# One matmul of 512 columns for both activation parts in the second half of an expert table, with the two partial results added on VectorE

## The chip, the cores and the metric

The kernel runs on one core of one Trainium2 chip. The metric is the device time of one execution in microseconds (us); the time before is the median of three runs. TensorE has two rows in the profile: PE is the stream of matmuls, PEld the loading of their stationary operands. VectorE is DVE, ScalarE is ACT, GpSimd is POOL, SyncE is SP and issues the DMAs.

## The reference

Two layers of an encoder over 256 positions with 1024 channels. Each layer mixes the positions (attention, a long convolution, a Fourier mixing) and then adds a retrieval of single-neuron experts, which is where most of the time goes. This change touches only the first table of the retrieval, `u_tab`:

```python
s = jnp.einsum('thpd,phkd->thpk', q, sub_keys)      # 8 heads, two halves of 128 keys
...                                                 # top 16 of 16 x 16 pairs: idx, gates g
ue = jnp.take(u_tab, ib, axis=0)
a = jax.nn.gelu(jnp.einsum('thkd,td->thk', ue, xb), approximate=False)
ve = jnp.take(v_tab, ib, axis=0)
return jnp.einsum('thk,thkd->td', (gb * a).astype(ve.dtype), ve)
```

There are 128 x 128 experts. The kernel does not gather: it multiplies all 16384 rows of both tables, and sets the weight of what was not picked to zero.

## The kernel before

Everything is float32, but TensorE is fed in the form fp32r, which keeps fewer bits. So each operand is split in an upper part (`_hi`, a rounded copy made by ScalarE) and a lower part (`_lo`, the original minus the upper part), and each product is three matmuls: upper by lower, upper by upper, lower by upper. The fourth, lower by lower, is left out.

**Tiles.** One layer streams 296 tiles of weights, of 128 x 1024 elements, through four slots `raw`. ScalarE copies each half tile (128 x 512) to `tab_hi`, and GpSimd or VectorE subtracts it to give `tab_lo`. `tab_hi` and `tab_lo` have two slots each, so half a tile can be split as soon as TensorE has used the same half of the tile two before it (semaphore `half_used`). Tiles 40 to 167 of the stream are the 128 tiles of the first table (`u_tile`), the last 128 those of the second (`v_product`).

**A tile of the first table.** Its result is 128 experts by 256 positions. For each of 8 blocks of 128 channels, `u_tile` issues a matmul of `x_lo` and two of `x_hi`, each with a moving operand of 256 columns; all add up in one half of a bank of PSUM (`ps`). Two tiles (a pair) fill a bank. ScalarE then applies GELU to the pair (`gelu` into `work`, from tile 48 on `gelu_in_place` in PSUM).

**The gate stage, tiles 48 to 111.** By tile 48 the picks are known. Between the tiles TensorE makes the gates out of one-hot matrices, four positions at a time: 64 groups, one after each tile (`gates`; 4 float32 matmuls, shown as x8, in a bank of their own). Their operands come from VectorE (`hot_rows` L1586, `hot_columns` L1591 for every second group) and from ScalarE (`distances` L1110 and `one_hot_j` L1118 for the others). VectorE multiplies each finished group into `work` (`weigh_group`, L1598), and multiplies each pair after its GELU into `work` too (`gate_pair`, L1606). GpSimd makes `tab_lo` (`u_lower`, L1239). In what follows a tile whose number in a quad is even opens a pair, and an odd one closes it.

**The tail, tiles 112 to 127.** No gates are made, and VectorE makes `tab_lo` (L1567). The second table follows at once: `v_product` waits for `w_lo` (L1660) of its tile, then for `tab_lo` (L1652). Both stand in one queue on VectorE, behind everything issued before.

Every engine runs its own instructions in the order in which they are written, with semaphores between them. No scheduler decides anything. In the gate stage ScalarE's order for a pair is: distances, split of the two halves of the even tile, one-hot, split of the two halves of the odd tile, GELU of the pair that ended last.

## Time and profile before

| | |
|---|---|
| median of 3 runs | 2057.51 us (2055.43 to 2057.92) |
| the profiled execution | 2052.14 us, span 2050.3 us |
| PE busy | 1958.4 us, 96% of the span |
| PEld busy | 1786.3 us, 87% |
| DVE busy | 1320.7 us, 64% |
| ACT busy | 1103.0 us, 54% |
| POOL busy | 770.4 us, 38% |

A matmul's duration is from its start to its modelled end, and neighbours overlap; how fast matmuls follow each other is read from their starts. In layer 0 the gate stage lies at about 381 to 622 us of the span, the tail at 622 to 668, the second table at 668 to 1023; layer 1 repeats this.

### The profile page before, as it was taken

To read this page: it belongs to the slowest core of one execution; us is meant where nothing else is said; L and a number is where in the kernel's file an instruction comes from. 1 tells how busy PE (TensorE), PEld (TensorE's weight loads), DVE (VectorE), ACT (ScalarE), POOL (GpSimd) and SP (SyncE) were. 2 spreads that over 40 slices of the span, in tenths; PEclk is the share of its full clock that TensorE was granted. 3 is DMA by queue.
4 is the path that set the end of the run, shared out by engine and by line. 5 is a ranking of instruction groups with operands and counts; after the bars stand their busy time and mean duration, and the time that the engine had idled before them with its cause. 6 is when DMAs were issued, how large, how long until landed. Compare 5 with 4: busy or idle time off the path is not lost.

```text
span 2050.3 us, 43061 instructions
## 1 busy us (share of the span) xinstructions
PE 1958.4 (96%) x12792; PEld 1786.3 (87%) x12792; DVE 1320.7 (64%) x2869; ACT 1103.0 (54%) x2124; POOL 770.4 (38%) x553
## 2 busy tenths in 40 slices
PE   7989998999999999999998999989999999999997
PEld 6779997999999887888777799979999998878886
DVE  4655699666666665666546557986666666656665
ACT  4344454666665554555533454546666555555554
POOL 4433599576770000000054316995777600000000
PEclk9999999999999999999999999999999999999999
DMA  5215454444344556555522154544343455565555
GB/s 209 74 42 174 153 178 144 153 143 140 137 142 173 187 194 235 192 194 194 185 73 82 55 182 150 179 145 151 134 143 135 141 178 191 194 244 194 194 190 179
DMA packets 90470, 327.05 MB, mean 160 GB/s; under 512 B 10400, under 2 KB 11168, under 8 KB 89760
## 3 DMA queue, kind: packets, MB, share of 16 engines
q1 hardware_dynamic: 90400, 326.18, 46.0%
q8 instruction: 36, 0.59, 0.1%
q14 instruction: 34, 0.28, 0.0%
HBM read 325.09 MB, written 1.05 MB: 159 GB/s over the span
## 4 chain that ended last, share of the span: by engine, by line
PE 88%; DVE 5%; issue 3%; POOL 2%; DMA 1%; ACT 1%; SPq 1%; DVEq 0%; POOLq 0%; ACTq 0%
PE ps L795 12%; PE ps L796 12%; PE ps L797 12%; PE ps L868 11%; PE ps L871 11%; PE ps L870 11%; PE ps L814 6%; PE ps L768 2%; PE ps L771 1%; PE ps L770 1%; POOL tab_lo L1239 1%; DVE work L1345 1%; DMA raw<-tab_v 1%; PE ps L579 1%; PE ps L545 1%
## 5 line engine op out<-in xcount | busy, mean ns | idle before, releaser
L1239 POOL TENSOR_TENSOR tab_lo<-raw,tab_hi 128x512 fp32r<-128x512 f32 x416 | 586.3, 1425 | 262.0 <-ACT tab_hi L1071 181.2
L795 PE MATMUL ps<-x_lo,tab_hi 128*128 128x256 f32 x2048 | 591.8, 289 | 22.1 <-POOL tab_lo L1239 18.9
L797 PE MATMUL ps<-x_hi,tab_lo 128*128 128x256 f32 x2048 | 579.1, 283 | 0.0
L796 PE MATMUL ps<-x_hi,tab_hi 128*128 128x256 f32 x2048 | 579.0, 283 | 0.0
L1652 DVE TENSOR_TENSOR tab_lo<-raw,tab_hi 128x512 fp32r<-128x512 f32 x512 | 354.2, 692 | 280.0 <-ACT tab_hi L1166 276.2
L1071 ACT ACTIVATE tab_hi<-raw 128x512 fp32r<-128x512 f32 x504 | 317.5, 631 | 338.9 <-PE ps L797 334.4
L795 PEld LDWEIGHTS ps<-x_lo,tab_hi 128*128 128x128 f32 x2048 | 392.0, 191 | 25.7 <-POOL tab_lo L1239 25.4
L868 PE MATMUL ps<-tab_lo,w_hi 128*128 128x512 f32 x1024 | 400.6, 391 | 7.5 <-DVE w_lo L1660 7.5
L870 PE MATMUL ps<-tab_hi,w_hi 128*128 128x512 f32 x1024 | 399.8, 390 | 0.0
L871 PE MATMUL ps<-tab_hi,w_lo 128*128 128x512 f32 x1024 | 399.8, 390 | 0.0
L796 PEld LDWEIGHTS ps<-x_hi,tab_hi 128*128 128x128 f32 x2048 | 392.5, 192 | 0.0
L797 PEld LDWEIGHTS ps<-x_hi,tab_lo 128*128 128x128 f32 x2048 | 391.9, 191 | 0.0
L1166 ACT ACTIVATE tab_hi<-raw 128x512 fp32r<-128x512 f32 x512 | 319.0, 624 | 103.6 <-PE ps L871 92.8
L868 PEld LDWEIGHTS ps<-tab_lo,w_hi 128*128 128x128 f32 x1024 | 193.3, 189 | 49.0 <-DVE tab_lo L1652 9.2
L871 PEld LDWEIGHTS ps<-tab_hi,w_lo 128*128 128x128 f32 x1024 | 193.1, 189 | 40.5
L870 PEld LDWEIGHTS ps<-tab_hi,w_hi 128*128 128x128 f32 x1024 | 193.3, 189 | 40.1
L1156 ACT ACTIVATE w_hi<-work 128x256 fp32r (+1 forms) x256 | 106.8, 417 | 199.9 <-PE ps L871 198.5
L1598 DVE TENSOR_TENSOR work<-ps,work 128x512 f32 (+1 forms) x128 | 88.6, 692 | 157.3 <-PE ps L814 157.3
L1187 POOL TENSOR_TENSOR small<-small,kc 128x2 f32<-128x2 f32 x10 | 6.9, 692 | 451.9 <-DVE small L1279 434.8
L895 ACT ACTIVATE tab_hi<-raw 128x512 fp32r<-128x512 f32 (+1 forms) x168 | 100.3, 609 | 131.4 <-PE ps L771 47.4
L1586 DVE TENSOR_SCALAR onehot<-kc,picks 128x128 f32<-128x128 f32 x512 | 168.2, 388 | 0.6
L1194 POOL TENSOR_TENSOR tab_lo<-raw,tab_hi 128x512 fp32r<-128x512 f32 (+1 forms) x96 | 121.5, 1277 | 117.8 <-ACT tab_hi L895 116.5
(204 smaller groups left out, 2527.5 us busy)
## 6 DMA issues: line engine op xcount, KB each, us to landing
raw<-tab_u SPq DMA_DIRECT2D x256, 512.0 KB, 3.2
raw<-tab_v SPq DMA_DIRECT2D x256, 512.0 KB, 3.2
raw<-w_proj SPq DMA_DIRECT2D x68, 512.0 KB, 3.5
raw<-w_proj SPq DMA_DIRECT2D x16, 384.0 KB, 3.1
work<-cdft SPq DMA_DIRECT2D x3, 1536.0 KB, 9.5
work<-cfilter SPq DMA_DIRECT2D x3, 768.0 KB, 5.4
work<-sub_keys SPq DMA_DIRECT2D x2, 1024.0 KB, 5.5
work<-pmat SPq DMA_DIRECT2D x3, 352.0 KB, 6.2
```

The lines of the kernel that those rows point to most:

```text
L795: mm(bank, hi, x_lo[:, 4 * h + k, :], start=(h + k == 0), stop=False)
L796: mm(bank, hi, x_hi[:, 4 * h + k, :], start=False, stop=False)
L797: last = mm(bank, lo, x_hi[:, 4 * h + k, :], start=False, stop=(h + k == 4))
L814: last = mm(ps[:, 2 + s, t * P:(t + 1) * P], onehot[:, s % 2, 0, t, :], onehot[:, s % 2, 1, t, :], start=True, stop=True)
L868: mm(bank, w_hi[:, s % 2, tok], lo, start=(first and s == 0), stop=False, skip_group_check=True)
L870: mm(bank, w_hi[:, s % 2, tok], hi, start=False, stop=False, skip_group_check=True)
L871: last = mm(bank, w_lo[:, s % 2, tok], hi, start=False, stop=last_tile, skip_group_check=True)
L1071: fn(half(tab_hi, s, h), half(raw, s, h), ACT.Copy).then_inc(hi_done.sem, 1)
L1166: fn(half(tab_hi, s, h), half(raw, s, h), ACT.Copy).then_inc(hi_done.sem, 1)
L1239: tt(half(tab_lo, s, h), half(raw, s, h), half(tab_hi, s, h).bitcast(F32), ALU.subtract).then_inc(lo_pool.sem, 1)
L1586: last = v.tensor_scalar(onehot[:, slot, 0, t, :], iota, picks[:, 0, bass.ds(n * 4 + t, 1)], picks[:, 2, bass.ds(n * 4 + t, 1)], ALU.is_eq ...
L1652: v.tensor_tensor(half(tab_lo, s, h), half(raw, s, h), half(tab_hi, s, h).bitcast(F32), ALU.subtract).then_inc(lo_dve.sem, 1)
```

## The change

For tiles 48 to 127 the upper part of the table is multiplied with both activation parts in one matmul. `x_hi` and `x_lo` become two views of one tensor `x_hl`, in which the 256 upper and 256 lower columns of a channel block lie side by side. The result of the 512 columns fills a whole bank: the left half holds the upper product, and the product of `tab_lo` with `x_hi` is added there, while the right half holds the product with `x_lo`. The two halves have to be added, which a new step `sum_pair` does on VectorE for each pair, out of PSUM into a new SBUF tensor `sums`. GELU then works in `sums` and waits for that step; `gate_pair` reads `sums` instead of PSUM and is moved one tile later. A pair takes two banks (0 and 1, or 2 and 3), and the gates go to banks 4 to 7.

```diff
-        x_hi = sb("x_hi", [P, DT, SEQ], F32R)
-        x_lo = sb("x_lo", [P, DT, SEQ], F32R)
+        x_hl = sb("x_hl", [P, DT, 2, SEQ], F32R)
...
+        sums = sb("sums", [P, 2, 2, SEQ])
...
+                def u_tile_joint(i, s, signal, offset):
+
+                    j = i * 4 + s
+                    for h in range(2):
+                        pe.wait_ge(*at(signal, l, j * 2 + offset + h + 1))
+                        for k in range(4):
+                            col = slice(k * P, (k + 1) * P)
+                            hi, lo = half(tab_hi, s, h)[:, col], half(tab_lo, s, h)[:, col]
+                            mm(ps[:, s, :], hi, x_hl[:, 4 * h + k, :, :].rearrange("p a t -> p (a t)"),
+                               start=(h + k == 0), stop=False, skip_group_check=True)
+                            last = mm(ps[:, s, 0:256], lo, x_hi[:, 4 * h + k, :], start=False, stop=(h + k == 4),
+                                      skip_group_check=True)
+                        last.then_inc(half_used.sem, 1)
...
-                        if s % 2 == 0:
-                            pe.wait_ge(*at(gated, l, i * 2 + s // 2 - 1 - GATE0 // 2))
-                        u_tile(i, s, lo_dve, LO_T)
+                            pe.wait_ge(*at(summed, l, i * 2 + s // 2 - 1 - GATE0 // 2))
+                        u_tile_joint(i, s, lo_dve, LO_T)
...
                 def gelu_in_place(n, bank):
-                    act.wait_ge(*at(half_used, l, n * 4 + 2 * U0 + 4))
-                    fn(ps[:, bank, :], ps[:, bank, :], ACT.Gelu).then_inc(gelu_done.sem, 1)
+                    act.wait_ge(*at(summed, l, n - GATE0 // 2 + 1))
+                    fn(sums[:, bank, :, :], sums[:, bank, :, :], ACT.Gelu).then_inc(gelu_done.sem, 1)
...
+                def sum_pair(n, bank):
+
+                    dve.wait_ge(*at(half_used, l, n * 4 + 2 * U0 + 4))
+                    v.tensor_reduce(sums[:, bank, :, :],
+                                    ps[:, 2 * bank:2 * bank + 2, :].rearrange("p k (a t) -> p k t a", a=2),
+                                    AX.X, ALU.add).then_inc(summed.sem, 1)
...
                         if s == 0 and not first:
+                            sum_pair(i * 2 - 1, 1)
+                        if s == 1 and not first:
                             gate_pair(i * 2 - 1, 1, n)
                             dve.wait_ge(*at(gated, l, i * 2 - GATE0 // 2))
                         if s == 2:
+                            sum_pair(i * 2, 0)
+                        if s == 3:
                             gate_pair(i * 2, 0, n)
                             dve.wait_ge(*at(gated, l, i * 2 + 1 - GATE0 // 2))
...
-                        if s % 2:
+                        if s % 2 == 0:
+                            sum_pair(i * 2 + s // 2 - 1, (s // 2 + 1) % 2)
+                        else:
                             gate_pair(i * 2 + s // 2 - 1, (s // 2 + 1) % 2, GROUPS)
...
                 dve.wait_ge(*at(weighted, l, GROUPS))
+                sum_pair(63, 1)
                 v_quad(0, True)
```

In the order of instructions this stands as follows. VectorE in the first quad of the gate stage, before: the work of three groups, where `work<-ps,work 128x128x4` is `weigh_group` and `work<-ps,work 128x512` is `gate_pair`.

```order
L1598 TENSOR_TENSOR work<-ps,work 128x128x4
L1586 TENSOR_SCALAR onehot<-kc,picks 128x128 x4
L1591 TENSOR_TENSOR onehot<-kc,picks 128x512
L1603 REGISTER_ALU
L1606 TENSOR_TENSOR work<-ps,work 128x512
L1623 ISA
L1596 REGISTER_ALU
L1598 TENSOR_TENSOR work<-ps,work 128x128x4
L1586 TENSOR_SCALAR onehot<-kc,picks 128x128 x4
L1596 REGISTER_ALU
L1598 TENSOR_TENSOR work<-ps,work 128x128x4
```

The same place after the change; line numbers are 16 higher, and `sums<-ps` is `sum_pair`.

```order
L1614 TENSOR_TENSOR work<-ps,work 128x128x4
L1602 TENSOR_SCALAR onehot<-kc,picks 128x128 x4
L1607 TENSOR_TENSOR onehot<-kc,picks 128x512
L1619 REGISTER_ALU
L1620 TENSOR_REDUCE sums<-ps 128x512
L1612 REGISTER_ALU
L1614 TENSOR_TENSOR work<-ps,work 128x128x4
L1602 TENSOR_SCALAR onehot<-kc,picks 128x128 x4
L1626 REGISTER_ALU
L1629 TENSOR_TENSOR work<-sums,work 128x512
L1649 ISA
L1614 TENSOR_TENSOR work<-ps,work 128x128x4
```

The sum has taken the place of `gate_pair` behind the one-hot columns, and `gate_pair` stands one group later. VectorE where the tail ends and the second table begins, before: the last split of the tail, then the first tile of the second table, then the last `gate_pair`.

```order
L1567 TENSOR_TENSOR tab_lo<-raw,tab_hi 128x512
L1603 ISA
L1606 ISA
L1606 TENSOR_TENSOR work<-ps,work 128x512
L1646 REGISTER_ALU
L1646 COMPARE_AND_BRANCH
L1650 REGISTER_ALU
L1651 REGISTER_ALU
L1652 TENSOR_TENSOR tab_lo<-raw,tab_hi 128x512
```

And after the change:

```order
L1583 TENSOR_TENSOR tab_lo<-raw,tab_hi 128x512
L1626 ISA
L1629 ISA
L1629 TENSOR_TENSOR work<-sums,work 128x512
L1674 REGISTER_ALU
L1674 COMPARE_AND_BRANCH
L1619 REGISTER_ALU
L1620 TENSOR_REDUCE sums<-ps 128x512
L1678 REGISTER_ALU
L1679 REGISTER_ALU
L1680 TENSOR_TENSOR tab_lo<-raw,tab_hi 128x512
```

The sum of the last pair, which waits for the end of tile 127, now stands ahead of both splits of the second table's first tile and of its `w_lo`.

## Rows read from the trace of the kernel before

**Rows 1.** The page: busy us and share of each engine.

```profile
PE 1958.4 (96%) x12792; PEld 1786.3 (87%) x12792; DVE 1320.7 (64%) x2869; ACT 1103.0 (54%) x2124; POOL 770.4 (38%) x553
```

**Rows 2.** Chain that ended last, layer 0's gate stage: start us, us, what.

```profile
384.00 0.89 PE ps L814 x8
...
621.29 0.89 PE ps L814 x8
```

**Rows 3.** Timeline of PE, tail and second table: start us, us, line.

```profile
654.78 0.28 PE L795 MATMUL ps<-x_lo,tab_hi 128*128 128x256 f32 x1
...
657.66 0.28 PE L795 MATMUL ps<-x_lo,tab_hi 128*128 128x256 f32 x1
...
672.23 0.40 PE L868 MATMUL ps<-tab_lo,w_hi 128*128 128x512 f32 x1
...
674.96 0.39 PE L868 MATMUL ps<-tab_lo,w_hi 128*128 128x512 f32 x1
```

**Rows 4.** Timeline, gate stage: one pair, and ScalarE's rows of another.

```profile
508.87 0.58 ACT L1102 ACTIVATE ps<-ps 128x512 f32<-128x512 f32 x1
...
510.78 0.63 ACT L1071 ACTIVATE tab_hi<-raw 128x512 fp32r<-128x512 f32 x1
...
546.54 0.58 ACT L1102 ACTIVATE ps<-ps 128x512 f32<-128x512 f32 x1
...
546.61 0.36 PE L795 MATMUL ps<-x_lo,tab_hi 128*128 128x256 f32 x1
...
546.98 0.69 DVE L1598 TENSOR_TENSOR work<-ps,work 128x512 f32 x1 [1.81 <-PE ps L814]
...
548.33 0.63 ACT L1071 ACTIVATE tab_hi<-raw 128x512 fp32r<-128x512 f32 x1
...
548.78 0.68 DVE L1591 TENSOR_TENSOR onehot<-kc,picks 128x512 f32<-128x512 f32 x1
...
549.03 1.56 POOL L1239 TENSOR_TENSOR tab_lo<-raw,tab_hi 128x512 fp32r<-128x512 f32 x1 [1.03 <-ACT tab_hi L1071]
...
549.38 0.68 DVE L1606 TENSOR_TENSOR work<-ps,work 128x512 f32 x1
```

**Rows 5.** Groups by line and form: the reductions of VectorE.

```profile
L1556 DVE TENSOR_REDUCE chosen<-work 128x128 f32<-128x2048 f32 x8 | 18.3, 2286 | 0.3
...
L1376 DVE TENSOR_REDUCE small<-ps 128x4 f32<-128x1024 f32 x8 | 9.8, 1220 | 1.5 <-PE ps L657 1.3
```

**Rows 6.** Timeline of POOL, gate stage: one split, and two in a row.

```profile
500.07 1.28 POOL L1239 TENSOR_TENSOR tab_lo<-raw,tab_hi 128x512 fp32r<-128x512 f32 x1 [0.94 <-ACT tab_hi L1071]
...
503.83 2.83 POOL L1239 TENSOR_TENSOR tab_lo<-raw,tab_hi 128x512 fp32r<-128x512 f32 x2 [1.03 <-ACT tab_hi L1071]
```

**Rows 7.** Chain, 346 to 352 us: GpSimd's slowest split and PE behind it.

```profile
347.60 3.32 POOL tab_lo L1239
...
350.96 0.38 PE ps L795
```

**Rows 8.** Timeline of ACT, tail: last split of a pair's end, then GELU.

```profile
656.78 0.63 ACT L1071 ACTIVATE tab_hi<-raw 128x512 fp32r<-128x512 f32 x1 [0.81 <-PE ps L797]
...
657.32 0.58 ACT L1102 ACTIVATE ps<-ps 128x512 f32<-128x512 f32 x1
```

**Rows 9.** Timeline where the second table begins.

```profile
667.00 0.42 DVE L1660 TENSOR_TENSOR w_lo<-work,w_hi 128x256 fp32r<-128x256 f32 x1
...
667.98 0.28 PE L797 MATMUL ps<-x_hi,tab_lo 128*128 128x256 f32 x1
...
668.10 0.40 PE L868 MATMUL ps<-tab_lo,w_hi 128*128 128x512 f32 x1
...
671.43 0.49 PE L868 MATMUL ps<-tab_lo,w_hi 128*128 128x512 f32 x1 [0.43 <-DVE w_lo L1660]
```

**Rows 10.** Windows: busy us (instructions) by engine, granted clock, DMA share, GB/s.

```profile
802.00:806.00 4.00, 3.08 (x7) 2.48 (x8) 2.28 (x5) 1.15 (x4) 0.00 (x0) 0.50 0.65 230
806.00:812.00 6.00, 6.00 (x22) 4.79 (x21) 2.41 (x4) 2.65 (x6) 0.00 (x0) 0.78 0.25 83
```

More of the change, by code:

```diff
@@ L123, in hybrid_encoder @@
         dist_abs = sb("dist_abs", [P, 4, P])
+        sums = sb("sums", [P, 2, 2, SEQ])
         ps = ctx.enter_context(nc.psum_tensor("ps", [P, 8, 512], F32))
+        x_hi, x_lo = x_hl[:, :, 0, :], x_hl[:, :, 1, :]
         workf = work[:, :, :].rearrange("p j t -> p (j t)")
@@ L311, in hybrid_encoder @@
         unit_set = sig("unit_set", 3)
+        summed = sig("summed", (P - GATE0) // 2)
         gated = sig("gated", (P - GATE0) // 2)
@@ L813, in gates @@
                     for t in range(4):
-                        last = mm(ps[:, 2 + s, t * P:(t + 1) * P], onehot[:, s % 2, 0, t, :],
+                        last = mm(ps[:, 4 + s, t * P:(t + 1) * P], onehot[:, s % 2, 0, t, :],
                                   onehot[:, s % 2, 1, t, :], start=True, stop=True)
@@ L820, in u_gates @@
                         if s % 2 == 0:
-                            if first:
-                                pe.wait_ge(*at(gelu_done, l, i * 2 + s // 2 - 1))
-                            else:
-                                pe.wait_ge(*at(gated, l, i * 2 + s // 2 - 1 - GATE0 // 2))
-                        u_tile(i, s, lo_pool, LO_G)
+                            if not first:
+                                pe.wait_ge(*at(summed, l, i * 2 + s // 2 - 1 - GATE0 // 2))
+                            elif s == 0:
+                                pe.wait_ge(*at(gelu_done, l, i * 2))
+                        u_tile_joint(i, s, lo_pool, LO_G)
                         gates(i, s, first)
@@ L830, in u_tail @@
                         if s % 2 == 0:
-                            pe.wait_ge(*at(gated, l, i * 2 + s // 2 - 1 - GATE0 // 2))
-                        u_tile(i, s, lo_dve, LO_T)
+                            pe.wait_ge(*at(summed, l, i * 2 + s // 2 - 1 - GATE0 // 2))
+                        u_tile_joint(i, s, lo_dve, LO_T)
                 u_product(0, True, lo_pool, LO_E)
@@ L1605, in gate_pair @@
                     pair = work[:, bass.ds(2 * n, 2), :]
-                    v.tensor_tensor(pair, ps[:, bank, :].rearrange("p (k t) -> p k t", k=2), pair, ALU.mult)\
-                        .then_inc(gated.sem, 1)
+                    v.tensor_tensor(pair, sums[:, bank, :, :], pair, ALU.mult).then_inc(gated.sem, 1)
                 def gate_quad(i, first=False, last=False):
@@ L1626, in gate_quad @@
                             u_lower_half(i + 1, 0, 1)
-                        weigh_group(n, 2 + s)
+                        weigh_group(n, 4 + s)
                 hot_rows(0, 0)
@@ L1794 @@
     from concourse.bass_utils import run_bass_kernel_spmd
-    nc = bacc.Bacc("TRN2", target_bir_lowering=False, num_devices=1)
+    nc = bacc.Bacc("TRN2", target_bir_lowering=False, num_devices=1, dynamic_dma_scratch_size=1024)
     arrays = layouts(inputs)
```

## The prediction

> **What bounds the kernel now.** I read the page first. PE is busy for 96% of the span, DVE for 64% and POOL for 38% [rows 1], so TensorE is the first suspect. A busy PE is not yet a bound one, so I then followed the chain that ended last through the gate stage. It never leaves PE there: the gates of the 64 groups start from 384.00 to 621.29, 63 steps of 3.767 us [rows 2], so a pair of tiles takes 7.53 us. What such a period is made of I took from the starts of matmuls, not from their durations. In the tail nine groups of three lie within eight gaps, from 654.78 to 657.66: 24 matmuls of 256 columns in 2.88 us, 0.120 each. In the second table 12 matmuls of 512 columns take 2.73 us, 0.2275 each [rows 3]. A tile of 24 matmuls is therefore 2.88 us and the gates after it 0.89. Last I read the timeline of one pair, to see what each other engine does between the end of a pair and the start of the next but one [rows 4]. That decides this case.
>
> **What TensorE saves.** For each channel block two matmuls of 256 columns (0.240) become one of 512 (0.2275), and the third stays at 0.120. The saving is 0.0125 to 0.0135 us; I take 0.0133, since 256 columns at 0.120 and 512 at 0.227 lie on one line whose fixed part is 0.0133 a matmul. That is 8 x 0.0133 = 0.107 us a tile, and 17.0 us for 160 tiles (80 in each layer) if nothing else moves. A pair in the gate stage would take 7.53 - 0.21 = 7.32.
>
> The trace's cadence is weighed here against a rule. The Trainium skill, "TensorE: Matmul & The Clock Gate", section "Back-to-back issue gap", puts the gap at N/2.4 + 2.5 ns, so that a matmul saved would be worth only 2.5 ns and the change would save 3 us instead of 17. This case's trace has 0.120 for 256 columns where that rule gives 0.109. I go by the trace.
>
> **What VectorE gets.** 80 sums of 1024 values read from PSUM. The nearest row is a reduction of 1024 PSUM values to 4 in 1.220 us; one of 2048 values to 128 takes 2.286 [rows 5], so the price follows the values read, not the results. This one writes 512 results where the rows write 4 and 128. Bounds: 0.69, what an operation with 512 results takes [rows 4], and 2.29, the row with twice the values. I take 1.22, whose row has the values and the memory that this one has. VectorE has room for it: it waits 1.81 before one of the two groups of each pair [rows 4].
>
> **The new chain.** The sum itself is hidden from TensorE, whose banks it frees more than a tile early. But GELU now waits for it, and behind GELU in ScalarE's queue stand the distances and then the split of the even tile of the pair after next, for which GpSimd and then TensorE wait. Before, GELU ran the moment the pair was done: it starts 0.54 after the last split starts [rows 8], at 546.54 in the pair I follow, ahead even of the next tile's first matmul at 546.61 [rows 4]. Now, counted from that first matmul:
> - the gate group is weighed at 546.98, and what follows the one-hot columns of 548.78 starts at 549.38 [rows 4]: the sum starts at +2.77
> - sum 1.22, hand-over 0.03 (an estimate: the hand-over of GpSimd to TensorE below is 0.04): GELU starts at +4.02
> - from the start of GELU to the start of the split 1.79 (546.54 to 548.33) in one pair and 1.91 (508.87 to 510.78) in the next [rows 4], mean 1.85: split at +5.87
> - split 0.63 and 0.07 to the start on GpSimd (548.33 to 549.03) [rows 4]: +6.57
> - GpSimd 1.28 [rows 6]: +7.85
> - TensorE takes over 0.04 later (347.60 + 3.32 = 350.92, PE at 350.96) [rows 7]: the even tile of the pair after next can start at +7.89.
>
> So from the end of pair p to the start of pair p+2 there are 7.89 us, and that pair takes 7.32. The second half of that tile comes a little late too: two splits in a row take 2.83 [rows 6], which ends it at 6.57 + 2.83 = +9.40, and TensorE is through with the first half (four blocks at 0.227 + 0.120 = 0.347, 1.39) at +9.28, so 0.12. Two periods last 7.89 + 7.32 + 0.12 = 15.33, one 7.665 us, against 7.53 before. TensorE's gain of 0.21 is eaten by a wait of 0.345, and each pair is 0.132 slower.
>
> **The other places.** In each layer the first two pairs of the gate stage have no late GELU before them and keep their gain, 2 x 0.21 = 0.43. The tail's 16 tiles keep theirs, 1.71: after the end of an odd tile (656.78, when its last split can start [rows 8]) the sum ends 1.25 later and GELU starts; the split it delays is wanted only 5.5 us after. Splits there are on VectorE, 0.69 each, and fit.
>
> At the start of the second table VectorE's queue now has the last sum ahead of both splits and `w_lo`. Before, `w_lo` was started at 667.00, a us before tile 127 ended, and the second table began at 668.10, 0.12 after the last matmul of the first [rows 9]. Now the sum starts when that matmul ends, 667.98 + 0.28 + 0.04 = 668.30, and after it come two splits and `w_lo`: 1.22 + 2 x 0.61 + 0.42 = 2.86, TensorE at about 671.2, that is 3.1 later. Its second tile starts at 671.2 + 2.73 = 673.9, where before it started at 671.43 after a wait of its own [rows 9]: the cost is 2.5.
>
> Bank 0 of the gate stage now waits for the last GELU of the stage before at once; the picks, which TensorE waits for anyway, come later than that, so it costs nothing. Were that cover gone, it would be part of one GELU, 0.58 [rows 4]. The wider `x_hl` changes no matmul elsewhere: each still reads 256 columns that lie together.
>
> **The sum.** Per layer: 30 pairs x 0.132 = +4.0, -0.43, -1.71, +2.5, so +4.3; two layers +8.6. The profiled execution of 2052.1 (span 2050.3, 1.8 around it; 5.4 under the median of the runs) would become 2060.7, and the median of 2057.5 becomes 2066.1. I say 2066. A measurement of this kernel can tell about 0.2%, 4.1 us.
>
> **The rivals.**
> - *The chain is shorter, and TensorE's gain comes through (faster).* Each 0.1 us off the chain is 0.05 a pair, 3.0 us over 60 pairs. If the sum cost 0.69, by results, a pair would take 7.40 and the total be -7.8 in the 60 pairs, -0.9 in the other four, -3.4 in the tails, +4.0 at the starts of the second table, -8.1: 2049.5. If the chain dropped out altogether (0.69 off), -13.6 - 3.4 + 5.0 = -12: 2045.5. The change turns from loss to gain where the chain is 0.29 shorter, at a sum of 0.93 us. For it: the chain is put together from rows of other places, and some of it may overlap. Against it: the row for 1024 values from PSUM is exact. Chance 0.15.
> - *The chain is 0.15 to 0.42 shorter (no change within 0.2%).* 2053.5 to 2061.5, worked out in the same way. Chance 0.10.
> - *GpSimd is slowed by what now runs beside it.* `gate_pair` reads both inputs from SBUF where one came from PSUM, and it starts near +5.95, right before GpSimd's split at +6.57; also GpSimd now works where the one-hot columns are built. In the rows GpSimd took 1.56 instead of 1.28 for a split that began during the columns [rows 4, 6], and 3.32 at worst beside long operations of VectorE [rows 7]. 0.28 more in the chain is +8.4: 2074.5; a whole 0.68 is +20: 2086. It decides once GpSimd's first split is late by 0.1. Chance 0.15. The Trainium skill, "SBUF — State Buffer", section "Who interferes with whom", says that such an instruction of VectorE and one of GpSimd that reads SBUF exclude each other, and that a reduction never does; by that rule the new form of `gate_pair` is a new rival for GpSimd and the sum is not, and the 1.56 agrees that columns do slow it.
> - *The clock falls at the start of the second table.* The new gap is 3.1 us. After the long wait for a DMA in the second table of layer 0 the granted clock was 0.50 in one window and 0.78 in the next, which is 1.2 GHz for the first and part of the second, and 29 matmuls ran in 10 us [rows 10] where 44 fit: 15 x 0.2275 = 3.4 us lost. Twice, +6.8: 2073. Chance 0.10.
>
> A sum of 2.29 would be 1.07 more in the chain, +32, with +2 at the starts of the second table: 2100. It has no row that speaks for it and no chance of its own here. By the Trainium skill's issue gap a pair in the gate stage would take 7.49 without waits and 7.75 with them, and the kernel would end at about 2075 (an estimate from that page).
>
> **How the numbers follow.** Forecast 0.50, own range 2060 to 2072 (0.06 of it within 0.2%); rivals 0.15, 0.10, 0.15, 0.10. Faster: 0.15 + 0.02 = 0.17. Within 0.2%: 0.06 + 0.08 = 0.14. Slower: 0.44 + 0.15 + 0.10 = 0.69. The range leaves out the fastest half of the first rival and the slow end of the third: 2052 to 2079.
>
> **What would show it.** In the profile after: starts of the joint matmul and the next 0.227 apart, then 0.120; 160 reductions of about 1.22; gates every 7.6 to 7.7 us per pair; PE idle some 0.35 per pair before the first matmul of even tiles, released by GpSimd's `tab_lo`, some 20 us in all; GELU about 4 us after the next tile's start; tail tiles at 2.77; a wait of about 3 us for `w_lo`, twice. The prediction is wrong if PE has no wait in the gate stage (then it is faster), or if GpSimd's mean there rises well over the 1.3 of single splits.

## The result, and the profile after

The changed kernel takes 2161.88 us (median of 4 runs, 2159.32 to 2167.99) where the kernel before takes 2056.47 beside it (4 runs, 2055.11 to 2057.92): 1.0517 times as long, 95% interval 1.0493 to 1.0541. Slower was forecast, but by 0.4%, not by 5.2%; 2161.88 lies far outside 2052 to 2079.

First the page of the changed kernel: busy us and share of the span by engine.

```profile
PE 1968.4 (91%) x11512; PEld 1726.4 (80%) x11512; DVE 1578.0 (73%) x2949; ACT 1077.0 (50%) x2124; POOL 749.3 (35%) x553
```

PE has 1280 matmuls fewer than in [rows 1], as the change says. VectorE has 80 instructions more, but is busy for 257 us more, where 80 sums of 1.22 make 98. The other 159 must be in instructions that were there before. The page's costliest groups say which (busy us, mean ns of one, then idle time before them and who ended it):

```profile
L810 PE MATMUL ps<-x_hl,tab_hi 128*128 128x512 f32 x1280 | 465.9, 405 | 97.5 <-POOL tab_lo L1255 93.9
...
L1602 DVE TENSOR_SCALAR onehot<-kc,picks 128x128 f32<-128x128 f32 x512 | 344.3, 732 | 0.8
...
L1118 ACT ACTIVATE sums<-sums 128x512 f32<-128x512 f32 x80 | 50.7, 633 | 318.8 <-DVE sums L1620 318.8
```

L1602 is `hot_rows`, which builds the one-hot rows for the gates and which the diff doesn't touch. Before, the page has it as L1586:

```profile
L1586 DVE TENSOR_SCALAR onehot<-kc,picks 128x128 f32<-128x128 f32 x512 | 168.2, 388 | 0.6
```

388 ns became 732 in the mean, and that is 176 us more of VectorE (other groups give 16 us back). The sum itself costs what it should; this is its group by form:

```profile
L1620 DVE TENSOR_REDUCE sums<-ps 128x512 f32<-128x1024 f32 x80 | 97.1, 1214 | 22.2 <-PE ps L812 22.2
```

The timeline of one pair in the gate stage shows where the rows lose it. VectorE first (start us, us, engine, line):

```profile
506.10 4.37 DVE L1602 TENSOR_SCALAR onehot<-kc,picks 128x128 f32<-128x128 f32 x4
510.38 0.68 DVE L1607 TENSOR_TENSOR onehot<-kc,picks 128x512 f32<-128x512 f32 x1
510.98 1.21 DVE L1620 TENSOR_REDUCE sums<-ps 128x512 f32<-128x1024 f32 x1
...
512.72 1.10 DVE L1602 TENSOR_SCALAR onehot<-kc,picks 128x128 f32<-128x128 f32 x4
...
520.24 1.21 DVE L1620 TENSOR_REDUCE sums<-ps 128x512 f32<-128x1024 f32 x1
```

Then ScalarE and GpSimd over the same stretch:

```profile
502.98 0.63 ACT L1118 ACTIVATE sums<-sums 128x512 f32<-128x512 f32 x1 [4.85 <-DVE sums L1620]
503.51 1.27 ACT L1126 ACTIVATE dist_abs<-kc,chosen 128x128 f32<-128x128 f32 x4
504.69 1.13 ACT L1087 ACTIVATE tab_hi<-raw 128x512 fp32r<-128x512 f32 x2
...
506.25 1.14 ACT L1087 ACTIVATE tab_hi<-raw 128x512 fp32r<-128x512 f32 x2
...
512.23 0.63 ACT L1118 ACTIVATE sums<-sums 128x512 f32<-128x512 f32 x1 [4.85 <-DVE sums L1620]
```

```profile
505.38 5.00 POOL L1255 TENSOR_TENSOR tab_lo<-raw,tab_hi 128x512 fp32r<-128x512 f32 x4 [4.25 <-ACT tab_hi L1087]
```

Four rows take 1.10 when GpSimd is idle (512.72) and 4.37 when it splits the table (506.10), and the instruction behind the slow four starts at 510.38, the moment GpSimd's run of four splits ends. In shorter windows the view shows them one by one:

```profile
506.61 1.29 POOL L1255 TENSOR_TENSOR tab_lo<-raw,tab_hi 128x512 fp32r<-128x512 f32 x1
506.66 1.32 DVE L1602 TENSOR_SCALAR onehot<-kc,picks 128x128 f32<-128x128 f32 x1
...
507.90 1.33 DVE L1602 TENSOR_SCALAR onehot<-kc,picks 128x128 f32<-128x128 f32 x1
```

A row that starts 0.05 after a split ends with that split, 1.32 later instead of 0.33. So a run of splits without a gap holds one row after the other. In the kernel before, four rows took 1.17 to 1.36 in the same stretch:

```profile
506.18 1.33 DVE L1586 TENSOR_SCALAR onehot<-kc,picks 128x128 f32<-128x128 f32 x4
```

Its splits came singly or in twos [rows 6]. The two that began at 503.83 ended at 506.66, and of the four rows only the first was held, for 0.57.

The three lists close into a ring (each link is released by the one before, and the last releases the first), which I read off by starts: GELU at 502.98, GpSimd 2.40 later, behind the distances and the first split of ScalarE; its run, 5.00; the columns after it, 0.60; the sum and the hand-over to the next GELU, 1.25. That is 9.25, with no time left over: it is the distance from GELU to GELU (502.98 to 512.23) and from sum to sum (510.98 to 520.24). A pair takes 9.25 where it took 7.53 [rows 2]. TensorE only follows. In the list of waits (us in total, times, longest)

```profile
PE ps L810 <- POOL tab_lo L1255: 93.9, 60, 1.9
```

it waits 60 times, about once a pair, as ScalarE waited 80 times for the sum, 318.8 us in all (the third row of the groups above). In windows of the same 211 us (busy us by engine, in the order PE, PEld, DVE, ACT, POOL, then granted clock, DMA share, GB/s) VectorE was at 140.9 before, in the first line, and is at 205.6 now, in the second. It is hardly ever free, and is held for 3.27 of each 9.25 us (4.37 less 1.10):

```profile
409.00:620.00 211.00, 211.00 (x1795) 211.00 (x1794) 140.91 (x337) 133.79 (x276) 146.89 (x110) 1.00 0.40 139
...
409.00:620.00 211.00, 174.32 (x1093) 153.53 (x1092) 205.60 (x298) 101.32 (x230) 113.59 (x91) 1.00 0.34 112
```

Outside the gate stage most went as forecast. In the tail the sums are 5.55 us apart, 2.775 a tile. TensorE then waits 2.93 for the second table, and behind that comes what only a rival had: the granted clock, 1.00 through the gate stage and the tail, is at 0.50 (1.2 GHz). Timeline and windows at the start of the second table in layer 0:

```profile
683.35 1.23 DVE L1620 TENSOR_REDUCE sums<-ps 128x512 f32<-128x1024 f32 x1 [1.31 <-PE ps L812]
688.90 1.23 DVE L1620 TENSOR_REDUCE sums<-ps 128x512 f32<-128x1024 f32 x1 [1.31 <-PE ps L812]
...
716.63 1.23 DVE L1620 TENSOR_REDUCE sums<-ps 128x512 f32<-128x1024 f32 x1 [2.51 <-PE ps L812]
...
718.98 0.42 DVE L1688 TENSOR_TENSOR w_lo<-work,w_hi 128x256 fp32r<-128x256 f32 x1
719.53 0.79 PE L884 MATMUL ps<-tab_lo,w_hi 128*128 128x512 f32 x1 [2.93 <-DVE w_lo L1688]
```

```profile
719.50:723.00 3.50, 3.47 (x8) 2.80 (x9) 2.04 (x4) 0.88 (x2) 0.00 (x0) 0.50 0.66 176
723.00:726.30 3.30, 3.30 (x10) 2.54 (x10) 0.97 (x2) 1.05 (x3) 0.00 (x0) 0.59 0.34 132
726.30:730.00 3.70, 3.70 (x18) 3.05 (x17) 2.27 (x5) 1.88 (x4) 0.00 (x0) 1.00 0.38 144
```

Matmuls of 512 columns start 0.427 apart for 6.1 us, so some 14 of them cost 0.2 more each, 2.9 us. In layer 1 the gap is 2.93 again, and the slow starts end after 3.7 us (1794.19 to 1797.89): some 9 matmuls, 1.7 us.

The account of the two profiled executions (2162.92 against 2052.14, +110.8), from starts on TensorE: first gates to last gates of layer 0 took 287.5 (383.07 to 670.55) against 237.3 (383.83 to 621.13), +50.2; from there to the second table 48.98 against 46.97, +2.0, in which the tail gives back its 1.7, so that the gap and what is late around it cost 3.7; then 2.9 for the clock. That is 55.1. In layer 1 the gates took 288.0 (1457.18 to 1745.21) against 237.3, the way to the second table is the same 48.98, and the clock cost 1.7: 54.4. Together that is 109.5 of the 110.8.

### The profile page after: what moved, and what is told of

Read it like the earlier page. It is cut to its first block, busy times and chain, and to the rows that moved or that the text cites. A ratio compares the mean times of both kernels' runs of the same rounds, so it can differ in the third digit from the quotient of the medians.

```text
span 2160.9 us, 40655 instructions
## 1 busy us (share of the span) xinstructions
PE 1968.4 (91%) x11512; PEld 1726.4 (80%) x11512; DVE 1578.0 (73%) x2949; ACT 1077.0 (50%) x2124; POOL 749.3 (35%) x553
## 4 chain that ended last, share of the span: by engine, by line
PE 63%; DVE 22%; issue 6%; DVEq 2%; ACT 2%; POOL 2%; DMA 1%; SPq 0%; POOLq 0%; ACTq 0%
DVE onehot L1602 12%; PE ps L884 10%; PE ps L886 10%; PE ps L887 10%; PE ps L797 4%; PE ps L799 4%; PE ps L798 4%; PE ps L810 3%; DVE sums L1620 3%; PE ps L812 2%; ACT sums L1118 2%; DVE work L1629 2%; PE ps L770 1%; PE ps L773 1%; PE ps L772 1%
## 5 line engine op out<-in xcount | busy, mean ns | idle before, releaser
L1255 POOL TENSOR_TENSOR tab_lo<-raw,tab_hi 128x512 fp32r<-128x512 f32 x416 | 565.5, 1387 | 388.5 <-ACT tab_hi L1087 307.5
L810 PE MATMUL ps<-x_hl,tab_hi 128*128 128x512 f32 x1280 | 465.9, 405 | 97.5 <-POOL tab_lo L1255 93.9
L1087 ACT ACTIVATE tab_hi<-raw 128x512 fp32r<-128x512 f32 x504 | 301.1, 622 | 175.9 <-PE ps L799 147.8
L1182 ACT ACTIVATE tab_hi<-raw 128x512 fp32r<-128x512 f32 x512 | 319.2, 624 | 106.3 <-PE ps L887 96.0
L810 PEld LDWEIGHTS ps<-x_hl,tab_hi 128*128 128x128 f32 x1280 | 240.3, 188 | 160.9 <-POOL tab_lo L1255 109.1
L812 PE MATMUL ps<-x_hl,tab_lo 128*128 128x256 f32 x1280 | 358.0, 280 | 0.0
L1602 DVE TENSOR_SCALAR onehot<-kc,picks 128x128 f32<-128x128 f32 x512 | 344.3, 732 | 0.8
L812 PEld LDWEIGHTS ps<-x_hl,tab_lo 128*128 128x128 f32 x1280 | 241.6, 189 | 0.0
L797 PE MATMUL ps<-x_hl,tab_hi 128*128 128x256 f32 x768 | 219.2, 285 | 18.9 <-POOL tab_lo L1255 18.9
L798 PE MATMUL ps<-x_hl,tab_hi 128*128 128x256 f32 x768 | 217.3, 283 | 0.0
L799 PE MATMUL ps<-x_hl,tab_lo 128*128 128x256 f32 x768 | 217.2, 283 | 0.0
L1118 ACT ACTIVATE sums<-sums 128x512 f32<-128x512 f32 x80 | 50.7, 633 | 318.8 <-DVE sums L1620 318.8
L797 PEld LDWEIGHTS ps<-x_hl,tab_hi 128*128 128x128 f32 x768 | 147.3, 192 | 21.9 <-POOL tab_lo L1255 21.7
```

Source lines behind the costliest of these rows:

```text
L797: mm(bank, hi, x_lo[:, 4 * h + k, :], start=(h + k == 0), stop=False)
L798: mm(bank, hi, x_hi[:, 4 * h + k, :], start=False, stop=False)
L799: last = mm(bank, lo, x_hi[:, 4 * h + k, :], start=False, stop=(h + k == 4))
L810: mm(ps[:, s, :], hi, x_hl[:, 4 * h + k, :, :].rearrange("p a t -> p (a t)"), start=(h + k == 0), stop=False, skip_group_check=True)
L812: last = mm(ps[:, s, 0:256], lo, x_hi[:, 4 * h + k, :], start=False, stop=(h + k == 4), skip_group_check=True)
L1182: fn(half(tab_hi, s, h), half(raw, s, h), ACT.Copy).then_inc(hi_done.sem, 1)
```

## The experiments

The first theory after reading this: the rows are held by GpSimd's splits because both read SBUF (*the lock*), and the ring feeds on it. The rival: it is my own chain, only longer, or plain load on VectorE.

**rows_from_psum.** The 128 numbers that every one-hot row is compared with are put in a PSUM bank, and `hot_rows` reads them there. To free a bank, the gates of all four groups of a quad use banks 4 and 5 in turn.

```diff
+                v.tensor_copy(ps[:, 6, 0:P], iota)
...
-                        last = v.tensor_scalar(onehot[:, slot, 0, t, :], iota, picks[:, 0, bass.ds(n * 4 + t, 1)],
+                        last = v.tensor_scalar(onehot[:, slot, 0, t, :], ps[:, 6, 0:P], picks[:, 0, bass.ds(n * 4 + t, 1)],
...
-                        weigh_group(n, 4 + s)
+                        weigh_group(n, 4 + s % 2)
```

> The changed kernel, but VectorE's one-hot rows read their 128 columns of iota from a PSUM bank instead of SBUF (so the gates use two banks in turn instead of four). Lock theory (in the changed kernel each of the four row operations of a group waits until GpSimd has ended a split, because both want the same SBUF port): with one input in PSUM the four rows take 1.0 to 1.5 us again instead of 4.4, a pair in the gate stage takes 7.6 to 7.9 us instead of 9.25, and the kernel 2062 to 2085 us. Queue theory (VectorE's queue and the late GELU alone make the period, the long rows are only the place where the wait shows): rows stay long, pair 9.2, kernel about 2160.

2079.78 us (2 runs; before 2052.61), ratio 1.0133 [1.0103, 1.0162]: three quarters of the loss are gone. The gates' use of two banks instead of four was not run alone; it gives VectorE no work and takes none away, and gelu_behind_both below does without it. Groups and timeline of this kernel:

```profile
L1603 DVE TENSOR_SCALAR onehot<-ps,picks 128x128 f32<-128x128 f32 x512 | 173.9, 402 | 0.8
...
L1608 DVE TENSOR_TENSOR onehot<-kc,picks 128x512 f32<-128x512 f32 x64 | 73.4, 1146 | 0.0
```

```profile
506.47 5.45 POOL L1255 TENSOR_TENSOR tab_lo<-raw,tab_hi 128x512 fp32r<-128x512 f32 x4 [2.44 <-ACT tab_hi L1087]
508.39 1.37 DVE L1603 TENSOR_SCALAR onehot<-ps,picks 128x128 f32<-128x128 f32 x4
509.68 1.11 DVE L1608 TENSOR_TENSOR onehot<-kc,picks 128x512 f32<-128x512 f32 x1
510.20 1.72 POOL L1255 TENSOR_TENSOR tab_lo<-raw,tab_hi 128x512 fp32r<-128x512 f32 x1
```

GpSimd still runs its four splits in one piece (506.47 to 511.92), and the rows in the middle of them take 1.37. So the run of splits by itself does not cost the 5%; rows that read SBUF beside it do. The columns, which read two inputs from SBUF, now fall into the run and take 1.11 where 0.68 is their time alone, and the split that starts in the middle of them (510.20, the last of the four) takes 1.72 instead of 1.28.

**rows_cols_from_psum.** The same, and `hot_columns` too reads the numbers from PSUM.

```diff
-                    v.tensor_tensor(onehot[:, 1, 1, :, :], iota.rearrange("p (a c) -> p a c", a=1).broadcast_to([P, 4, P]),
+                    v.tensor_tensor(onehot[:, 1, 1, :, :], ps[:, 6, 0:P].rearrange("p (a c) -> p a c", a=1).broadcast_to([P, 4, P]),
```

> As the kernel with the rows from PSUM, and the one-hot columns read iota from PSUM too, so that they have one input in SBUF instead of two. Lock theory: at or up to 10 us below the kernel with the rows alone, since splits that run beside columns cost GpSimd up to 0.3 us less. Queue theory: no difference to the changed kernel, about 2160.

2080.31 (2 runs), 1.0135 [1.0106, 1.0165]. The columns are back at their own time, and nothing is gained:

```profile
L1608 DVE TENSOR_TENSOR onehot<-ps,picks 128x512 f32<-128x512 f32 x64 | 43.5, 679 | 0.0
```

What is left, 27 us, is therefore not VectorE waiting for SBUF. The trace shows where the gain of the columns went. GELU comes earlier, and with it GpSimd's run, whose first split now starts beside `gate_pair` of VectorE, and TensorE waits for that split:

```profile
513.89 0.68 DVE L1630 TENSOR_TENSOR work<-sums,work 128x512 f32 x1
514.04 1.67 POOL L1255 TENSOR_TENSOR tab_lo<-raw,tab_hi 128x512 fp32r<-128x512 f32 x1 [2.48 <-ACT tab_hi L1087]
...
515.76 0.50 PE L810 MATMUL ps<-x_hl,tab_hi 128*128 128x512 f32 x1 [0.24 <-POOL tab_lo L1255]
```

In nine such groups of four splits the first took 1.62 to 1.77, the others 1.26 to 1.30. In rows_from_psum the columns are 0.43 longer and the first split is at 1.27 to 1.28; here it is the other way round, with 0.4 on the split. A pair takes 7.87 there and 7.84 here (247.84 and 246.96 us from first to last gates of layer 0, 31.5 pairs).

**before_gelu_after_columns.** Can the ring be made without the change? The kernel before, with no joint matmul and no sum; only GELU in the gate stage waits for the one-hot columns, which delays ScalarE's queue as the sum does.

```diff
+                def gelu_late(n, bank):
+                    act.wait_ge(*at(hot_j_dve, l, n - GATE0 // 2 + 2))
+                    gelu_in_place(n, bank)
...
-                    gelu_in_place(i * 2 - 1, 1)
+                    gelu_late(i * 2 - 1, 1)
```

> The kernel before, with one wait added: in the gate stage GELU of a pair waits until VectorE has made the one-hot columns of the next pair. No joint matmul, no sum. Lock theory: GELU later by about 3 us pushes ScalarE's splits together, GpSimd's four splits of a pair then run in one piece across the time of VectorE's rows, and rows and GpSimd lock each other: rows 3 to 4.4 us, pair about 8.0 to 8.1 us (the 9.25 of the changed kernel less the sum's 1.2), kernel about 2088. My prediction's chain without any lock: 6.7 + 7.5 us for two pairs is under two periods of 7.53, so no change, 2057.

2164.02 (2 runs), 1.0543 [1.0512, 1.0574]: as slow as the change, from one wait. My chain without a lock gave 2057 here and is out; the lock was expected at 2088, so its price was far too low. VectorE and GpSimd:

```profile
507.29 4.06 DVE L1590 TENSOR_SCALAR onehot<-kc,picks 128x128 f32<-128x128 f32 x4
...
507.42 5.08 POOL L1243 TENSOR_TENSOR tab_lo<-raw,tab_hi 128x512 fp32r<-128x512 f32 x4 [4.86 <-ACT tab_hi L1071]
```

Rows 4.06 and a run of four splits, as in the change. Here `gate_pair` also waits 0.93 for GELU in VectorE's own queue. The gates of layer 0 take 290.95 us from first to last (385.25 to 676.20), 9.24 a pair.

**before_gelu_after_pause.** The same, with a reduction of 1024 values behind the columns, for which GELU waits: the sum's load and its wait, without the joint matmul.

```diff
+                                v.tensor_reduce(pause[:, :], x[:, 0, :].rearrange("p (a k) -> p a k", a=4), AX.X,
+                                                ALU.add).then_inc(paused.sem, 1)
```

> The kernel before, with GELU waiting for a reduction of 1024 values (result unused) that VectorE makes after the one-hot columns: the timing of the change without its matmul. Lock theory: pair 9.2 to 9.3 us, rows 4.4, kernel 2155 to 2165, so the loss of the changed kernel is all there without the joint matmul. My prediction's chain without a lock: 7.89 + 7.53 + 0.12 for two pairs, 7.77 each, kernel 2071.

2230.98 (2 runs), 1.0869 [1.0838, 1.0901], a miss of some 70 us: `gate_pair` stands directly behind the reduction and waits for a GELU that waits for it. It is no clean copy of the change, which has a gate group between the sum and its `gate_pair`.

**sum_before_gates.** Back to the change. The sum is made before the odd tile's gates are weighed, half a tile earlier, so that by my chain the wait on GpSimd should vanish.

```diff
-                        if s == 2:
-                            sum_pair(i * 2, 0)
...
+                        if s % 2:
+                            sum_pair(i * 2 + s // 2, s // 2)
                         weigh_group(n, 4 + s)
```

**last_sum_later.** Only the last sum of a layer stands behind the first splits and `w_lo` of the second table. **both_moves** has both.

```diff
                         if first and s == 0:
+                            sum_pair(63, 1)
+                        if first and s == 1:
                             gate_pair(63, 1, GROUPS)
 
                 dve.wait_ge(*at(weighted, l, GROUPS))
-                sum_pair(63, 1)
```

> The changed kernel, with the sum of a pair moved in VectorE's queue to right before the multiplication of the pair's last gate group, where VectorE waited for TensorE, and the multiplication by GELU's result back to its old place. Lock theory: GELU is only 0.5 to 0.6 us later than in the kernel before, the splits of GpSimd lie as before, rows take 1.1 to 1.4, TensorE no longer waits in the gate stage: pair 7.32; tail saves 3.4, the start of the second table costs 5 for its gap and some 3 us each for the halved clock: 2057.5 - 13.6 - 3.4 + 5 + 6 = about 2051. If what costs is the load of VectorE and not the place of the sum: near 2160.

> The changed kernel, with only the last sum (tiles 126 and 127) moved behind VectorE's work for the first tile of the second table, and the last GELU and multiplication one tile later. Gap theory: the two waits of 2.9 us go, and with them the stretches of halved clock behind them (6 us at half speed each, 3 us lost): 10 to 12 us less than the changed kernel, 2150 to 2152. If the clock would have fallen anyway: 5 to 6 less.

> Both moves, the sum before the pair's last gates and the last sum behind the first tile of the second table. Lock theory with the gap: the full gain of the joint matmul, 160 tiles x 0.107 = 17 us: 2040 to 2042, 0.992 of the kernel before. Rival: VectorE, with 6.6 us of work in a pair of 7.3, still makes TensorE wait, 2045 to 2055.

Measured against 2053.82 of the kernel before: sum_before_gates 2142.41 (5 runs), 1.0429 [1.0409, 1.045]; last_sum_later 2155.25 (2 runs), 1.0491 [1.0464, 1.0518]; both_moves 2133.05 (5 runs), 1.0381 [1.0362, 1.0401]. The later last sum was expected to give 10 to 12 us. It gave about 5 alone (1.0517 to 1.0491, less than the two intervals, of 2 and 4 runs, can tell apart) and 9 beside the other move. What it was meant to do, it did: in last_sum_later the second table starts at 718.58 and its matmuls follow each other every 0.23 us at once, without the gap and without the slow clock. By the starts that is 9 us, 2.3 in each layer up to the second table and 4.6 for the clock; where the rest of it went, I can't say. The other move was a miss of 91 us, and both_moves, expected at 2040 to 2042, one of the same size. Here are ScalarE, GpSimd and VectorE of sum_before_gates:

```profile
497.83 0.64 ACT L1118 ACTIVATE sums<-sums 128x512 f32<-128x512 f32 x1 [4.50 <-DVE sums L1620]
...
500.23 5.26 POOL L1255 TENSOR_TENSOR tab_lo<-raw,tab_hi 128x512 fp32r<-128x512 f32 x4 [3.66 <-ACT tab_hi L1087]
...
501.44 4.14 DVE L1602 TENSOR_SCALAR onehot<-kc,picks 128x128 f32<-128x128 f32 x4
505.51 1.21 DVE L1620 TENSOR_REDUCE sums<-ps 128x512 f32<-128x1024 f32 x1
...
506.75 0.63 ACT L1118 ACTIVATE sums<-sums 128x512 f32<-128x512 f32 x1 [4.51 <-DVE sums L1620]
```

The ring has only lost the columns: 2.40 to GpSimd's start, 5.28 until the sum behind the held rows, 1.24 to GELU, 8.92. What feeds it, rows ahead of the sum and GELU ahead of the splits, is all there.

**gelu_behind_split** puts GELU behind the splits of the next even tile in ScalarE's queue; **gelu_behind_and_last_sum** adds the later last sum.

```diff
                     u_upper(i, 0)
+                    gelu_in_place(i * 2 - 2, 0)
                     one_hot_j(i, 0, False)
                     u_upper(i, 1)
-                    gelu_in_place(i * 2 - 1, 1)
```

> The changed kernel, with one change of order on ScalarE in the gate stage: GELU of a pair, which waits for VectorE's sum, stands behind the split of the next even tile instead of before it. Nothing on VectorE or GpSimd is changed. Loop theory (late sum, late GELU, late splits in one piece, GpSimd in one piece, rows held by GpSimd, late sum): the loop is cut between GELU and the splits, so rows take 1.1 to 1.4 us again, a pair in the gate stage 7.40 us, and only the start of the second table still costs (2.9 us of gap and about 3 us of halved clock, twice): ratio to the kernel before 0.998 to 1.002. If VectorE's load (the sum added) makes the period, rows and pair stay near 4.4 and 9.2: ratio 1.05.

> As the kernel with GELU behind the split, and the last sum moved behind VectorE's work for the first tile of the second table. 64 pairs x 0.13 and 32 tail tiles x 0.107: 8.3 + 3.4 = 12 us under the kernel before, ratio 0.994. If the start of the second table still costs, 0.997 to 1.0.

2139.94 (4 runs; before 2055.51), 1.0418 [1.0403, 1.0433], and 2135.36 (5 runs), 1.0394 [1.0379, 1.0409]: misses again. The odd tile's splits still stand behind GELU, and while GpSimd is late with them the even tile's queue up behind. In the first of the two, GpSimd starts 1.75 after GELU (503.29 to 505.04), its run takes 5.35, columns 0.61, sum and hand-over 1.24: 8.95. Half a cut doesn't open the ring.

**gelu_behind_both.** GELU stands behind the splits of both tiles, `gate_pair` one pair later, and the last sum is late; the rows read SBUF as in the change. If the ring is the cause, it is opened; if VectorE's load is, it stays.

```diff
                     one_hot_j(i, 0, False)
                     u_upper(i, 1)
-                    gelu_in_place(i * 2 - 1, 1)
+                    gelu_in_place(i * 2 - 2, 0)
...
                         if s == 1 and not first:
-                            gate_pair(i * 2 - 1, 1, n)
+                            gate_pair(i * 2 - 2, 0, n)
```

> The changed kernel, with GELU of a pair behind the splits of both tiles after next on ScalarE in the gate stage (the multiplication by its result one pair later on VectorE), and the last sum behind the first tile of the second table; rows and columns read iota in SBUF as before. ScalarE then never waits for VectorE's sum ahead of a split. Loop theory: full cut, pair 7.40, ratio to the kernel before 0.994 as with the rows from PSUM, though the rows still share the port. Load theory: pair 8.9, ratio 1.04.

**before_pause_only.** The reduction of before_gelu_after_pause in the kernel before, for which nothing waits: the load alone.

> The kernel before, with the reduction of 1024 values on VectorE after the one-hot columns of each pair (result unused), and nothing waiting for it. Loop theory (GELU and so the splits wait for VectorE, whose rows wait for the splits): without that wait the added 1.2 us are covered by VectorE's idle time and GpSimd's splits stay spread out; rows 1.1 to 1.5, pair 7.53 to 7.6, kernel as before within 0.5%. Load theory (1.2 us more on VectorE are enough): rows near 4, pair 9, kernel 2130 or more.

gelu_behind_both: 2057.28 (12 runs; before 2055.89), 1.0012 [1.0002, 1.0022]. before_pause_only: 2055.51 (10 runs), 1.0001 [0.9991, 1.0011]. So the load alone costs nothing in the kernel before, where VectorE has idle time (a row takes 474 ns there instead of 388, and that is covered too), and opening the ring takes 5% down to 0.1%, about 0.3% of it by the later last sum. It did not bring the 0.994 and the 7.40 a pair that were expected. Both kernels with the reduction also set `dynamic_dma_scratch_size=1024`, which by 1.0001 costs nothing. GpSimd and VectorE of gelu_behind_both, and its group of rows:

```profile
511.61 2.59 POOL L1255 TENSOR_TENSOR tab_lo<-raw,tab_hi 128x512 fp32r<-128x512 f32 x2 [1.40 <-ACT tab_hi L1087]
...
512.49 2.30 DVE L1602 TENSOR_SCALAR onehot<-kc,picks 128x128 f32<-128x128 f32 x4
...
517.04 1.67 DVE L1602 TENSOR_SCALAR onehot<-kc,picks 128x128 f32<-128x128 f32 x4
```

```profile
L1602 DVE TENSOR_SCALAR onehot<-kc,picks 128x128 f32<-128x128 f32 x512 | 249.1, 546 | 1.0
```

The splits come in twos again, and four rows take 1.67 to 2.30 instead of 4.37. They still lose 158 ns each against before. Sums are 7.65 apart (507.66 and 515.31). Between them VectorE waits once, for 0.23, and the window of the gate stage has it busy for 204 of 211 us:

```profile
409.00:620.00 211.00, 211.00 (x1331) 186.38 (x1332) 204.34 (x362) 135.38 (x272) 143.53 (x110) 1.00 0.41 139
```

**rows_psum_and_moves** joins rows_from_psum and both_moves; **all_cuts** joins rows_from_psum and gelu_behind_and_last_sum. Neither the rows nor my chain should then stand in the way.

> The changed kernel with the rows' iota in PSUM and the sum before the pair's last gates and the last sum behind the first tile of the second table. Here the loop is cut at the rows instead (they no longer wait for GpSimd) and GELU comes early: rows 1.4, pair 7.40, ratio 0.994. The same kernel with iota in SBUF had pairs near 8.9; if these stay, the lock is not in the rows.

> Rows' iota in PSUM, GELU behind the split, last sum later. If each cut alone frees TensorE, both together give nothing more: 0.994.

2041.31 (6 runs; before 2055.51), 0.9937 [0.9924, 0.995], and 2042.81 (4 runs), 0.9946 [0.9928, 0.9964]. Both were expected at 0.994, and both beat both kernels. A row takes 401 ns in rows_psum_and_moves. Here are its window, and two sums of all_cuts two pairs apart:

```profile
409.00:620.00 211.00, 211.00 (x1376) 190.96 (x1375) 179.24 (x370) 136.69 (x279) 154.98 (x112) 1.00 0.42 142
```

```profile
500.86 1.22 DVE L1621 TENSOR_REDUCE sums<-ps 128x512 f32<-128x1024 f32 x1
...
515.62 1.21 DVE L1621 TENSOR_REDUCE sums<-ps 128x512 f32<-128x1024 f32 x1
```

PE does 1376 matmuls in the 211 us where gelu_behind_both does 1331 (both count as busy throughout, so the busy time would not tell them apart), VectorE is at 179 instead of 204, and a pair takes 14.76 / 2 = 7.38. From first to last gates both take 232.12 us in each layer, against 237.30 before.

## Why the prediction was wrong

**The step that failed** is the first one of the new chain: "the gate group is weighed at 546.98, and what follows the one-hot columns of 548.78 starts at 549.38 [rows 4]: the sum starts at +2.77". It takes for granted that the rows between weighing and columns go on taking what they took before, though I was moving GpSimd's splits in time in the same paragraph. In the change the splits fall on the rows; four rows take 4.37, not 1.2; and since GELU and so the splits wait for what follows the rows, the delay returns as its own cause. A chain from pair p to p+2 became a ring from each pair to the next of 9.25 us. rows_from_psum takes the rows' source away from the splits, and 5.17% become 1.33%; before_gelu_after_columns makes the ring without sum or joint matmul; gelu_behind_both opens it with the rows left where they are; before_pause_only shows that a load like the sum's does not make it. The two half cuts fit too: their rings still close, with links that add up to 8.92 and 8.95 and leave no time between them. Of the prediction's own signs one spoke against it, though in another sense than it was meant: TensorE waited 93.9 us for GpSimd in front of the joint tiles, not some 20. GpSimd's mean, the other, did not rise.

It settles fast. In layer 0 of the changed kernel the first four rows of the stage take 3.15 (384.77; the kernel before has 3.15 there too), the next two groups of four 1.45 and 1.10, and then every second group is slow:

```profile
395.82 3.63 DVE L1602 TENSOR_SCALAR onehot<-kc,picks 128x128 f32<-128x128 f32 x4
...
404.24 4.46 DVE L1602 TENSOR_SCALAR onehot<-kc,picks 128x128 f32<-128x128 f32 x4
```

The kernel before shakes the same first collision off, and has at the same place:

```profile
396.83 1.35 DVE L1586 TENSOR_SCALAR onehot<-kc,picks 128x128 f32<-128x128 f32 x4
```

**The rival that was near** priced contention between the two engines, but the wrong way round and at the wrong instruction: GpSimd slowed by `gate_pair`, at +8 to +20. In the ring GpSimd was not: 5.00 for four splits. VectorE was. With the rows out of the way the rival comes true as it was written: in rows_cols_from_psum the split beside `gate_pair` takes 0.4 more, and the kernel 2080.31, between the 2074.5 and 2086 that it had for 0.28 and 0.68. The Trainium skill, "SBUF — State Buffer", section "Who interferes with whom", which I named for `gate_pair`, also says that `tensor_scalar` can use both of VectorE's port pairs, that GpSimd shares one of them, and that the one who comes second then waits for the whole instruction; an instruction of VectorE with one SBUF input outside those modes doesn't contend. By that rule the rows were the instruction to look at, and the traces agree: four rows alone 1.10, beside splits 4.37, beside splits with PSUM as source 1.37. It says as well that two SBUF inputs contend with GpSimd's reads, and the columns do: 1146 ns against 679 from PSUM, and the split behind them 1.72 against 1.28.

**What was right.** The sum: 1.22 forecast, 1.214 measured, by values read and not by results. The tail: 2.77 a tile, 2.775 measured. The last sum delaying the second table: 3.1 forecast, 2.93 measured. The place of the trouble, GELU behind the sum and the splits behind GELU, and the direction: with the rows out of SBUF the kernel is still 1.33% slower. The chain itself is seen when the rows are out of it: rows_from_psum runs at 7.87 a pair against 7.665 forecast, with PE waiting 0.3 at most in front of the joint tiles, each time for GpSimd. The chain is 0.4 longer than I had it, by the columns there and by the first split in rows_cols_from_psum, and by the prediction's own rule (0.05 a pair for each 0.1) 0.4 makes 7.665 into 7.87.

**What was mis-sized.** TensorE's gain in the gate stage: 0.21 a pair forecast, and 7.53 - 7.38 = 0.15 where nothing else bounds (all_cuts). The gain of 17.0 us over the kernel "if nothing else moves" would by that be some 13 (17.0 less 64 pairs x 0.06). By the starts in rows_psum_and_moves it is 13.8 (5.2 in the gate stage and 1.7 in the tail of each layer); the medians differ by 14.2. The fall of the clock at the second table was given a chance of 0.10 and happened in both layers, at 2.9 and 1.7 us where I had 3.4 each. The 3.4 was too large by its own rows: of the 10 us that it counts, TensorE was idle for 0.9 (3.08 busy of 4.00 [rows 10]). It need not have fallen, either: in rows_from_psum the gap in layer 0 is the same 2.93 (681.99), and the clock behind it stays at 1.00.

**What stays open.** That `gate_pair` holds the first split in rows_cols_from_psum is read from the trace; no run moves it away. And the 14 to 16 us between gelu_behind_both and the two fastest kernels fit the 158 ns that each row still loses, with VectorE's queue full; but that kernel differs from them in the order of GELU too, so this part is argued, not shown.

## What to carry to other kernels

When an edit makes a queue wait for another engine, follow the wait around until it comes back, and for each instruction on the way ask what will run beside it then, not what ran beside it before. Idle time on an engine says nothing of an instruction that can be held by a neighbour. Before pricing anything beside GpSimd, list which of VectorE's instructions read SBUF, and whether a small constant operand could lie in PSUM instead. If such a ring exists, move the waiting instruction behind all the work that others need from its queue; half of it is not enough here.

## What was unexpected of the hardware

- Four `tensor_scalar` rows of 128 fp32 elements took 1.10 us alone, 4.03 to 5.17 beside a run of four GpSimd splits, and 1.35 to 1.37 with the source in PSUM, beside the splits or not. A profile books the held time as busy.
- GpSimd's four splits took 5.00 while they held VectorE's rows. They took 5.45 when the rows ran from PSUM, because the fourth then stood beside the columns (1.72 instead of 1.28). In the ring only VectorE paid.
- One wait on ScalarE, with no other work added, cost 5.4% (before_gelu_after_columns); 64 reductions of 1.2 us on VectorE that nothing waited for cost nothing (before_pause_only, 1.0001).
- A gap of 2.93 us on TensorE was followed by a granted clock of 0.50 and then 0.59, and 1.00 from 726.30. The same gap in layer 0 of rows_from_psum was followed by 1.00 at once. The waits of 1.6 us in every pair of the gate stage left it at 1.00.
